# Conditioning products of a two-block transformer kernel gathered by batches in one PSUM bank

## What is computed

```python
for i in range(DEPTH):
    ml = (jax.nn.silu(c) @ w_mod[i] + b_mod[i]).reshape(B, N_MOD, 1, D)
    mc = (jax.nn.silu(c_ctx) @ w_mod[i] + b_mod[i]).reshape(N_MOD, D)
    hl = modulate(xl, ml[:, 0], ml[:, 1])     # rms_norm(x) * (1 + scale) + shift
    hc = modulate(xc, mc[0], mc[1])
    ...
    xl = xl + ml[:, 2] * ol
    xl = xl + ml[:, 5] * conv_ffn(modulate(xl, ml[:, 3], ml[:, 4]), ...)
```

## Time and profile before

| | us |
|---|---|
| median of 3 runs | 1980.78 (1979.58 to 1981.1) |
| span of the profiled execution, first to last instruction | 1975.9 |
| PE busy | 1791.5 (91%) |
| DVE busy | 1071.7 (54%) |
| ACT busy | 861.4 (44%) |
| mean granted clock of PE | 0.944 |

### The profile page before, as it was taken

One profiled execution on the slowest core, in us unless ns is written; L12 is line 12 of the kernel. 1 busy time (PEld: TensorE's weight loads), 2 busy tenths in 40 slices (PEclk: granted clock), 3 DMA queues, 4 the chain that ended last, 5 costly groups with the idle time before them and its releaser, 6 DMA issues.

```text
span 1975.9 us, 28057 instructions
## 1 busy us (share of the span) xinstructions
PE 1791.5 (91%) x11498; PEld 1549.8 (78%) x11498; DVE 1071.7 (54%) x1411; ACT 861.4 (44%) x1096; POOL 0.2 (0%) x4
## 2 busy tenths in 40 slices
PE   5989799987999879998788898899999979889998
PEld 5967799976897769997655667688888857679997
DVE  4334665458655665544835664554334464557754
ACT  5454454333433445433353562533233345456552
POOL 0000000000000000000000000000000000000000
PEclk9989899988998989999898999899999978989998
DMA  5655377743663037674310302122332223025552
GB/s 193 222 190 196 113 238 228 243 166 120 214 196 107 18 115 252 215 254 155 103 51 17 123 1 86 64 86 80 112 107 77 92 87 112 22 86 192 172 185 71
DMA packets 234657, 264.93 MB, mean 134 GB/s; under 512 B 4767, under 2 KB 208546, under 8 KB 234530
## 3 DMA queue, kind: packets, MB, share of 16 engines
q1 hardware_dynamic: 232866, 258.89, 40.5%
q10 hardware_dynamic: 1664, 4.26, 0.6%
HBM read 262.08 MB, written 1.05 MB: 133 GB/s over the span
## 4 chain that ended last, share of the span: by engine, by line
PE 81%; DVE 9%; ACT 7%; issue 2%; DMA 1%; DVEq 0%; ACTq 0%
PE ps L611 80%; ACT y L1162 2%; DVE wlo L1337 2%; ACT whi L920 1%; ACT uh L1165 1%; PE ps L854 1%; DVE y L1383 1%; DVE y L1594 1%; DVE ul L1587 1%; DVE small L1713 1%; DMA xin<-in_ctx 1%; DVE y L1611 1%; DVE rstd L1517 0%; DVE rstd L1515 0%; DVE sm L1707 0%
## 5 line engine op out<-in xcount | busy, mean ns | idle before, releaser
L611 PE MATMUL ps<-uh,whi 128*128 128x256 f32 (+1 forms) x2052 | 657.1, 320 | 60.6 <-DVE ul L1587 46.9
L1337 DVE TENSOR_TENSOR wlo<-raw,whi 128x2048 fp32r<-128x2048 f32 (+6 forms) x218 | 454.9, 2087 | 402.0 <-ACT whi L920 396.6
L611 PE MATMUL ps<-ul,whi 128*128 128x256 f32 (+1 forms) x2052 | 647.1, 315 | 0.0
L611 PE MATMUL ps<-uh,wlo 128*128 128x256 f32 (+1 forms) x2052 | 646.5, 315 | 0.0
L920 ACT ACTIVATE whi<-raw 128x2048 fp32r<-128x2048 f32 (+6 forms) x218 | 381.7, 1751 | 278.1 <-PE ps L611 226.7
L611 PEld LDWEIGHTS ps<-uh,whi 128*128 128x128 f32 x2052 | 402.5, 196 | 104.3 <-issue 71.3
L611 PEld LDWEIGHTS ps<-ul,whi 128*128 128x128 f32 x2052 | 402.9, 196 | 22.4 <-issue 2.2
L611 PEld LDWEIGHTS ps<-uh,wlo 128*128 128x128 f32 x2052 | 402.6, 196 | 21.1
L611 PE MATMUL ps<-hh,whi 128*128 128x256 f32 (+1 forms) x864 | 263.8, 305 | 0.0
L611 PE MATMUL ps<-hl,whi 128*128 128x256 f32 (+1 forms) x864 | 263.1, 305 | 0.0
L611 PE MATMUL ps<-hh,wlo 128*128 128x256 f32 (+1 forms) x864 | 263.1, 305 | 0.0
(11 more groups left out here) (214 smaller groups left out, 1853.8 us busy)
## 6 DMA issues: line engine op xcount, KB each, us to landing
raw<-in_w_mod SPq DMA_DIRECT2D x48, 1024.0 KB, 5.2
raw<-in_ffn_w_up SPq DMA_DIRECT2D x44, 1024.0 KB, 5.0
raw<-in_w_ff_in SPq DMA_DIRECT2D x32, 1024.0 KB, 5.6
raw<-in_w_ff_out SPq DMA_DIRECT2D x32, 1024.0 KB, 5.5
raw<-in_w_in_dil SPq DMA_DIRECT2D x18, 1024.0 KB, 5.1
raw<-in_w_in_sb SPq DMA_DIRECT2D x12, 1024.0 KB, 6.1
raw<-in_w_ple_gate SPq DMA_DIRECT2D x8, 1024.0 KB, 5.6
raw<-in_ffn_w_down SPq DMA_DIRECT2D x8, 896.0 KB, 4.5
```

The costliest lines, as they stand in the source:

```text
L611: return pe.matmul(out_, lhsT, rhs, start=start, stop=stop, skip_group_check=True)
L1337: nc.vector.tensor_tensor(wlo[:, s % SPLIT, 0:n], raw[:, c["r"] % RAW, 0:n], whi[:, s % SPLIT, 0:n].bitcast(F32), ALU.subtract).then_inc(* ...
```

## The change

The units' products are gathered by batches: units 0 to 11, 12 to 17 and 18 to 23 (`MOD_BATCHES`). All products of a batch accumulate in bank 7, unit by unit in rows of their own: `cc` now has 46 columns per k, zero but for columns 22 and 23, and the stationary operand of unit n is a window of 24 columns that starts at 22 - 2 (n - first), so that its pair of values falls on rows 2 (n - first) and 2 (n - first) + 1 of each 32-partition strip, and zeros on the other rows. Copy, turn and keep happen once per batch, in the place where those of its last unit (11, 17, 23) stood; the others return without an instruction. The turn goes to bank 6, with 24 moving columns of `select`. The first products of a batch wait for the copy of the batch before.

```diff
+MOD_ROWS = 24
+MOD_BATCHES = (0, 12, 18, 24)
...
     for q in range(4):
-        select[32 * q, 0] = select[32 * q + 1, 1] = 1.0
+        for m in range(MOD_ROWS):
+            select[32 * q + m, m] = 1.0
...
-        cc = sb("cc", [P, KD, 2])
+        cc = sb("cc", [P, KD, 2 * MOD_ROWS - 2])
...
-        select = select[:, 0:2]
+        select = select[:, 0:MOD_ROWS]
...
+        def mod_batch(n):
+
+            b = max(j for j, first in enumerate(MOD_BATCHES) if first <= n)
+            return MOD_BATCHES[b], MOD_BATCHES[b + 1]
+
+        def batch_ends(n):
+            return n + 1 in MOD_BATCHES
...
             def mod_products(n, pair):
 
-
-                if n >= 2:
-                    pe.wait_ge(*at("mod_kept", n - 2))
+                first, after = mod_batch(n)
+                r0 = MOD_ROWS - 2 - 2 * (n - first)
+                if n == first and n > 0:
+                    pe.wait_ge(*at("mod_rows", n - 1))
                 for half, c in enumerate(pair):
                     pe.wait_ge(landed[c["r"] % RAW], 16 * (c["r"] // RAW + 1))
                     for k in range(4):
-                        last = mm(ps[32 * k:32 * k + 2, 6 + n % 2, :], cc[:, half * 4 + k, :], raw[:, c["r"] % RAW, k * 512:(k + 1) * 512],
-                                  half == 0, half == 1)
+                        last = mm(ps[32 * k:32 * k + MOD_ROWS, 7, :], cc[:, half * 4 + k, r0:r0 + MOD_ROWS], raw[:, c["r"] % RAW, k * 512:(k + 1) * 512],
+                                  n == first and half == 0, n + 1 == after and half == 1)
                     last.then_inc(*up("weights_used", ("mod", c["r"])))
 
             def mod_turn(n):
+
+                if not batch_ends(n):
+                    return
                 pe.wait_ge(*at("mod_rows", n))
                 for j in range(4):
-                    last = mm(ps[:, 6 + n % 2, 2 * j:2 * j + 2], modrow[:, j * P:(j + 1) * P], select, True, True)
+                    last = mm(ps[:, 6, MOD_ROWS * j:MOD_ROWS * (j + 1)], modrow[:, j * P:(j + 1) * P], select, True, True)
                 last.then_inc(*up("mod_turned", n))
...
             def mod_rows(n, pair):
+                if not batch_ends(n):
+                    return
                 act.wait_ge(*at("weights_used", ("mod", pair[1]["r"])))
                 act.wait_ge(*own())
-                nc.scalar.activation(modrow, ps[:, 6 + n % 2, :], ACT.Copy).then_inc(*up("mod_rows", n))
+                nc.scalar.activation(modrow, ps[:, 7, :], ACT.Copy).then_inc(*up("mod_rows", n))
...
             def mod_keep(n):
-
-
-                l, c = divmod(n, 12)
-                dst = modc[:, l, 4 * c:4 * c + 4, :]
+                if not batch_ends(n):
+                    return
+                first, after = mod_batch(n)
+                l, c0, c1 = first // 12, first % 12, (after - 1) % 12 + 1
+                sums = ps[:, 6, 0:4 * MOD_ROWS].rearrange("p (j c s) -> p c j s", j=4, s=2)
+                dst = modc[:, l, 4 * c0:4 * c1, :].rearrange("p (c j) s -> p c j s", j=4)
+                base = bmod[:, l * 48 + 4 * c0:l * 48 + 4 * c1].rearrange("p (c j) -> p c j", j=4)
                 dve.wait_ge(*at("mod_turned", n))
                 for s_ in range(2):
                     dve.wait_ge(*own())
-                    nc.vector.tensor_tensor(dst[:, :, s_], ps[:, 6 + n % 2, s_:8:2], bmod[:, l * 48 + 4 * c:l * 48 + 4 * c + 4], ALU.add).then_inc(
-                        *up("vector_step"))
-                dve.wait_ge(*own())
-                nc.vector.tensor_scalar(dst, dst, 1.0 if c // 2 in (1, 4) else 0.0, None, ALU.add).then_inc(*up("mod_kept", n))
+                    nc.vector.tensor_tensor(dst[:, :, :, s_], sums[:, 0:c1 - c0, :, s_], base, ALU.add).then_inc(*up("mod_kept", n))
+                for which in (1, 4):
+                    if c0 <= 2 * which < c1:
+                        scales = modc[:, l, 8 * which:8 * which + 8, :]
+                        dve.wait_ge(*own())
+                        nc.vector.tensor_scalar(scales, scales, 1.0, None, ALU.add).then_inc(*up("mod_kept", n))
...
                     nc.vector.memset(small[:, :], EPS).then_inc(*up("vector_step"))
+                    nc.vector.memset(cc[:, :, :], 0.0).then_inc(*up("vector_step"))
```

More of the change, by code:

```diff
@@ L1448, in conditioning @@
                     dve.wait_ge(*own())
-                    nc.vector.tensor_tensor(cc[:, :, n], vec[:, ROW[name]:ROW[name] + 8], silu[:, n, :], ALU.mult).then_inc(
+                    nc.vector.tensor_tensor(cc[:, :, MOD_ROWS - 2 + n], vec[:, ROW[name]:ROW[name] + 8], silu[:, n, :], ALU.mult).then_inc(
                         *up("vector_step"))
```

## The result

The changed kernel takes 1958.84 us (median of 4 runs, 1957.98 to 1960.64), the kernel before 1980.18 us beside it (4 runs, 1979.27 to 1981.1): ratio 0.9893, 95% interval 0.9881 to 0.9904. Over all comparisons of the study before has a mean of 1980.26 us (68 runs) and after of 1959.01 us (8 runs). So the gain is 21.2 us, 1.1%. The forecast was 16.2 us, in a range whose lower end lay 1.2 us above what was measured.

The account below looks back on a forecast made before the run. PE was taken as the bound, waiting for nobody where the change works. Removing 21 of 24 turns saves 18.1 us, less 1.8 padding and 0.1 for wider keeps: 16.2 us, 1980.8 to 1964.6 us, range 1960 to 1971.

Parts of the forecast that it names:

- Isolated turns, 0.89 each: Turns between two ordinary groups (units 0, 8, 9, 10, 18, 19, 20, 14): removing each saves 0.89 us, 7.1 in all.
- late data: Rival: weights or mod chunks land too late, half the turns' gain is given back; 7 us gain, 1973.6 us, chance 0.07.
- Units 15 and 16, 0.72: Dilated queries and keys: each missing turn saves 0.72 us, the rotation's matmul needing its own 0.21 us entry; 1.4 in all.
- Units 12, 21, 22, 0.79: In ff_out, turns between a group and the next unit's products: 0.79 us saved each, 2.4 in all.
- Stick, 0.90: Stick attention, units 1 to 6: each missing turn saves 0.80 to 0.98 us, taken as 0.90, 5.4 in all.
- Unit 7, 1.1, and unit 13, 0.7: Last head's product starts 1.1 us sooner without the turn; at ff_out0's end, DVE's three small operations gone save 0.7 us.
- ACT and DVE at no cost: Removing 21 bank copies on ACT and 62 of 72 small DVE operations counts as nothing, apart from unit 13's place.
- Padding, 1.8: Products with 24 stationary columns instead of 2: only four loads per unit show, 0.08 us a unit, costing 1.8 us.
- The clock as noise of 2 us either way: PE's clock drops after each stage end, shifting with every change; allowed for as 2 us either way.
- Padding bare: Rival: all sixteen loads of each unit show their extra 19 ns; gain 10.7 us, time 1970.1 us, chance 0.12.
- slower: Rival: 24-column tiles no longer run beside each other, a unit takes 7.3 us; time 2094 us, chance 0.03.
- More than counted: Rival: stick entry at its lower bound, no padding cost, stage ends fall well; gain 20 us, 1960.5 us, chance 0.06.

Follow-up runs that it names:

- The run with thin products: The changed kernel with products streaming 2 moving columns of `raw` instead of 512, loads and waits kept, conditioning vectors not computed: 1924.44 us, ratio 0.9729.

## Why the prediction came out as it did

**The bound.** Right. PE waited for nobody in the stretches of the earlier trace rows, and there each turn taken from it came back as time at its own price. The run with thin products showed how much room was left. Units 14 and 15 lie outside these stretches, and there it does wait for chunks.

**Isolated turns, 0.89 each.** Seven of eight right (0.87 and 0.91, padding within). Unit 14 gave 0.56. Its turn came back in full: from the first matmul behind the products to the last of the group it is 11.88 us instead of 12.77. But the products of the unit take 2.23 to 2.36 us in the profiles of after's order with a short stretch ahead, instead of 1.83 to 2.10, since PE comes to them some 1.4 us sooner and then waits for the second chunk (the row at 448.32 above). With copies put back, where it comes late again, they take 1.85. So a small piece of the rival "late data" is in the result: 0.3 us, taken out of what the clock gave just before.

**Units 15 and 16, 0.72.** Too low: 0.87. The step that failed is the entry of its own for the rotation. With the turn gone the rotation's matmul follows an ordinary one after 0.12 us (507.98 to 508.10), not 0.21, and its own step is 0.46 instead of 0.54 (520.10 to 520.64 in before); the turn costs there what it costs elsewhere. In after:

```profile
508.10 1.02 PE L622 MATMUL ps<-qk,squares 128*128 128x512 f32 x2
508.56 0.68 PE L622 MATMUL ps<-uh,whi 128*128 128x256 f32 x1
```

**Units 12, 21, 22, 0.79.** Right, 0.77.

**Stick, 0.90.** Units 2 to 6 gave 0.96, so the value was the upper bound of 0.98 less the padding, not the middle: the direct entry from the head's product into the products costs what the entry into the turn cost, 0.80 us (147.15 to 147.95; in before 139.64 to 140.44). In after:

```profile
147.15 0.86 PE L622 MATMUL ps<-sba,v 128*64 128x256 f32 x4
147.95 1.92 PE L622 MATMUL ps<-raw,cc 128*24 128x512 f32 x16
149.79 0.48 PE L622 MATMUL ps<-q,k 64*128 64x256 f32 x1
```

The first pair gave 0.26 only. The turn itself gave its 0.98 there too, but unit 1's products, which begin at half clock, now have more of their length before the clock rises: their step to the next group is 2.83 us in after (125.14 to 127.97) where the repeated profile of before has 2.29 (126.08 to 128.37), and over all profiles 2.64 to 3.02 against 1.86 to 2.39. Together 5.1 for a forecast of 5.4.

**Unit 7, 1.1, and unit 13, 0.7.** Right in themselves: 1.15 and 0.65. But both stand at the end of a stage, and there the forecast stopped too early (below).

**ACT and DVE at no cost.** Right within the stages. The kept turns with 24 moving columns cost nothing either: from unit 11 to 12 25.88 us pass instead of 25.85, of which the padding is 0.02.

**Padding, 1.8.** The term was mis-sized: at most 0.5. The prediction let the four loads of a unit's first pass show. Measured is as much as the extra length of one load, about 20 ns, per unit; the other fifteen, the first pass's three among them, lie under other work. The earlier trace rows pointed that way, further than I followed it. The Trainium skill ("TensorE: Matmul & The Clock Gate", section "The mechanism") says that a load overlaps with matmuls in flight only if its row group differs. That sentence doesn't hold here: all tiles have the same 128 rows, and sixteen loads longer by 20 ns each cost 0.02 us together where bare they would cost 0.3.

**The clock as noise of 2 us either way.** This is the step that failed and that mattered. The sum of the steps without it is 17.5 us, which gives 1980.8 - 17.5 = 1963.3, inside the range. A further 3.4 us, which make it 1959.9, come from three stretches that PE passes at a higher clock than before: stick_out, the one behind its norm, and the one behind the norm of ff_out0. The first two go with turn 7 ahead of the last head, the third with keep 13 ahead of the last fold, and the runs that move or put back one of them alone show these links in the segments. The rows of one profile couldn't show the first, since in that execution stick_out ran at full clock. Its trace did show the third: a clock of 0.71 behind ff_out0. The forecast treated such changes as equally likely to help and to hurt and put their sum at nothing; these two pieces helped. That wasn't a law: the same move of keep 23 brought its 0.7 us and nothing behind ff_out1.

Why they act on the clock is open. Keep 13 lengthens a pause: PE stands still for 2.64 us ahead of the norm's matmul in before, and for 1.98 us with the keep behind the fold. Turn 7 doesn't: directly ahead of stick_out PE is idle for 1.09 us in after, with the turn put back (27.5 us) as without it (26.0 us). So the length of the pause isn't what decides in stick_out.

**The starting point.** The 4.9 us "outside the first and last instruction" were 1.8 us outside and some 2.5 to 3 us by which that execution was quicker than the median. It didn't touch the forecast, which took the same sum off the median, but it should have warned that the profile isn't the typical execution.

**The rivals.** Padding bare and slower fell by direct tests, and so did late data in the stretches that it was about. "More than counted" (1960.5) was nearest, and for its own reasons: the turns in the stick attention at their full 0.98, nearly no padding cost, and stage ends that fall well. It got a chance of 0.06.

## What to carry to other kernels

Where one engine is busy without a gap, small groups of instructions on it can be priced one by one from differences of starts, and the sum holds to a microsecond. A piece of work at the end of a stage, ahead of a pause of TensorE, can be worth more than its own length: at two of the three places here 0.7 to 1.2 us of it brought 1.3 to 2.7 us more through the clock, at the third nothing. So look at such places first and give them a term of their own, and test it by moving that one piece. Profile the kernel before more than once when the forecast rests on microseconds; one trace may be the odd one. And when single segments are compared, look at those that no edit touches too: here they moved by 1 to 3 us, and a sum that meets the total can hide that.

## What was not expected of the hardware

- A load of 24 columns took 104 ns against 83 for 2 and 192 for 128, and four column tiles with the same 128 rows still ran abreast with their loads hidden: 1.84 us for sixteen float32 passes of 512 moving columns with 24 stationary columns, 1.82 us with 2.
- One group of eight records (1 us) ahead of the last head decides in 13 of 14 profiles whether the following 26.0 us stage takes 27.5, and moving it or putting it back switches this. The idle time just ahead of the stage is 1.09 us either way in after.
- The same 777 matmul records of a stage took 145.7 or 148.4 us, never between in 14 profiles, in kernels that differ only hundreds of microseconds earlier. This stays unexplained.
